# Moving the layer-embedding products of a two-block transformer kernel to the three row-norm places, unsplit, with the results parked in device memory

## The reference, cut to what matters

```
out = merged @ w_o
x = x + gate * rms_norm(out, g_post)
```

```
x = layer_norm(alpha * x + y, ln_g[i], ln_b[i])            # y = attention output @ w_out
x = x + (p[i] @ w_ple[i]) * sigmoid(x @ w_ple_gate[i])     # p[i]: 256 x 256, w_ple[i]: 256 x 2048
```

## Time and profile before

| what | value |
|---|---|
| median of 3 runs | 2474.22 us (2472.71 to 2475.14) |
| the profiled execution's own time | 2475.72 us |
| its span (first to last instruction) | 2474.4 us |
| PE busy | 2372.7 us (96%) |
| DVE busy | 1496.3 us (60%) |
| ACT busy | 1133.7 us (46%) |
| POOL busy | 110.6 us (4%) |
| mean granted PE clock | 0.986 |
| DMA, mean | 190 GB/s |

### The profile page before, as it was taken

One profiled execution on the slowest core, in us unless ns is written; L12 is line 12 of the kernel. 1 busy time (PEld: TensorE's weight loads), 2 busy tenths in 40 slices (PEclk: granted clock), 3 DMA queues, 4 the chain that ended last, 5 costly groups with the idle time before them and its releaser, 6 DMA issues.

```text
span 2474.4 us, 28104 instructions
## 1 busy us (share of the span) xinstructions
PE 2372.7 (96%) x11204; PEld 1974.9 (80%) x11204; DVE 1496.3 (60%) x2082; ACT 1133.7 (46%) x1482; POOL 110.6 (4%) x120
## 2 busy tenths in 40 slices
PE   7899999989999999999998999999899999999988
PEld 4577888878888887888887888888788888888867
DVE  6887665444545445776755685566655456456664
ACT  4233444434444454453344444554455545455343
POOL 1000000000000000000000000000100011011010
PEclk9999999999999999999998999999899999999999
DMA  8886544535553457887564545555456555555544
GB/s 348 323 312 244 170 140 127 158 128 188 188 191 113 139 177 246 296 291 255 170 195 148 166 159 171 159 161 186 157 181 193 167 173 170 182 163 171 198 149 151
DMA packets 133542, 470.56 MB, mean 190 GB/s; under 512 B 15537, under 2 KB 15793, under 8 KB 132385
## 3 DMA queue, kind: packets, MB, share of 16 engines
q1 hardware_dynamic: 130688, 458.42, 56.4%
q0 software_dynamic: 1424, 9.37, 1.0%
q10 hardware_dynamic: 1298, 0.97, 0.1%
HBM read 466.60 MB, written 2.10 MB: 189 GB/s over the span
## 4 chain that ended last, share of the span: by engine, by line
PE 80%; DVE 6%; ACT 3%; issue 1%; DMA 1%; POOL 0%; DVEq 0%; ACTq 0%
PE G L466 24%; PE G L468 24%; PE G L467 24%; PE A L541 4%; DVE wlo L378 2%; PE A L791 1%; PE A L815 1%; ACT whi L376 1%; ACT dil L496 1%; PE A L991 1%; DMA raw<-in_weights 0%; DVE dil L1729 0%; PE A L1456 0%; DVE CP L1735 0%; PE A L957 0%
## 5 line engine op out<-in xcount | busy, mean ns | idle before, releaser
L378 DVE TENSOR_TENSOR wlo<-raw,whi 128x1024 fp32r<-128x1024 f32 (+2 forms) x782 | 937.3, 1202 | 743.3 <-ACT whi L376 740.9
L376 ACT ACTIVATE whi<-raw 128x1024 fp32r<-128x1024 f32 (+2 forms) x782 | 800.5, 1026 | 852.4 <-PE G L468 739.4
L466 PE MATMUL G<-whi,XH 128*128 128x512 f32 (+3 forms) x2804 | 1091.0, 389 | 29.7 <-DVE wlo L378 13.3
L468 PE MATMUL G<-whi,XL 128*128 128x512 f32 (+3 forms) x2804 | 1070.6, 382 | 0.0
L467 PE MATMUL G<-wlo,XH 128*128 128x512 f32 (+3 forms) x2804 | 1069.8, 382 | 0.0
L466 PEld LDWEIGHTS G<-whi,XH 128*128 128x128 f32 x2804 | 529.6, 189 | 129.3 <-DVE wlo L378 19.1
L468 PEld LDWEIGHTS G<-whi,XL 128*128 128x128 f32 x2804 | 528.8, 189 | 95.9
L467 PEld LDWEIGHTS G<-wlo,XH 128*128 128x128 f32 x2804 | 529.9, 189 | 90.5 <-issue 0.5
L328 DVE CUSTOM_DVE_ANT_0 raw<-raw,dil 128x1024 f32<-128x1024 f32 x64 | 84.9, 1339 | 10.4 <-DMA raw<-in_weights 10.4
L466 PE MATMUL A<-whi,XH 128*128 128x512 f32 x164 | 70.0, 427 | 6.3 <-DVE XL L643 3.4
L468 PE MATMUL A<-whi,XL 128*128 128x512 f32 x164 | 64.6, 394 | 0.0
(11 more groups left out here) (195 smaller groups left out, 1621.0 us busy)
## 6 DMA issues: line engine op xcount, KB each, us to landing
raw<-in_weights SPq DMA_DIRECT2D x792, 512.0 KB, 4.2
raw<-in_weights SPq DMA_DIRECT2D x80, 384.0 KB, 3.1
raw<-in_weights SPq DMA_DIRECT2D x16, 288.0 KB, 2.9
raw<-in_weights SPq DMA_DIRECT2D x8, 336.0 KB, 3.0
FT<-in_xT SPq DMA_DIRECT2D x4, 512.0 KB, 5.6
Xn<-in_x POOLq DMA_DIRECT2D x1, 2048.0 KB, 11.8
GG<-in_ln_g POOLq DMA_DIRECT2D x2, 1024.0 KB, 8.4
CP<-in_ln_b POOLq DMA_DIRECT2D x2, 1024.0 KB, 5.1
```

The source lines that it names most:

```text
L376: th = AC.mark(nc.scalar.activation(h[:, 0:2 * cols], r[:, 0:2 * cols], ACT.Copy))
L378: tl = VE.mark(nc.vector.tensor_tensor(l[:, 0:2 * cols], r[:, 0:2 * cols], h[:, 0:2 * cols].bitcast(F32), ALU.subtract))
L466: nc.tensor.matmul(o, h, wh, start=(k == start), stop=False)
L468: ins = nc.tensor.matmul(o, l, wh, start=False, stop=(k == nkt - 1))
```

## The change

The eight embedding slots leave `ple`. Two are multiplied at row-norm place 0, three at place 1 and three at place 2 (layer 1's first chunk at place 1), in the unsplit form, with `p` transposed on the host (`pT`) as the left side. `fill` copies each result to a `nat` buffer (ACT), and POOL writes that to a buffer in device memory, `spill`; `nat_done` gets the token of this write. `fill_before` puts one slot (place 0) or two (places 1 and 2) ahead of the first transposes, and one behind the transposes of the first four tiles. `ple` has POOL load each chunk into `PL`. `p_task` and the load of `p` go away; `pT` (512 KB) is loaded by POOL behind three other loads after the first attention phase. The planner counts 3.45 us for an unsplit slot, also for those of before. POOL's descriptor scratch is set to 8192.

```diff
+    fills = deque((f"w_ple{layer}", 512 * c, 512, 2) for layer in range(2) for c in range(4))
+    plan_gemm([fills.popleft() for _ in range(2)])
     plan_gemm([("w_a", 5120, 384, KT), ("w_a", 5504, 384, KT), ("w_a", 5888, 336, KT), ("w_a", 2048, 512, KT),
...
     out_seq("w_oa")
+    plan_gemm([fills.popleft() for _ in range(3)])
     plan_gemm(ple_seq(0))
...
     out_seq("w_ob")
+    plan_gemm(fills)
     plan_gemm(ple_seq(1))
...
+        whole = WHOLE | {s for s, n in enumerate(wslots) if plan[n][1] in ("w_ple0", "w_ple1")}
...
-            PE.wait(loaded[n] if s in WHOLE else split_done[s])
+            PE.wait(loaded[n] if s in whole else split_done[s])
+            full, full_ready = (FT, whole_ready) if s in WHOLE else (xh, ready)
...
-            PE.busy(12 * (cols + 32) / 2400.0)
+            PE.busy(3.45 if s in whole else 12 * (cols + 32) / 2400.0)
...
+        pT = sb("pT", [128, 4, T], F32, px)
...
+        d_pT = load(GP, "pT", pT[:, :, :], i["pT"])
...
+        def fill(count):
+
+            for _ in range(count):
+                layer, c = fills.popleft()
+                pair, t = gemm(512, 2, pT[:, 2 * layer:2 * layer + 2, :], None, [d_pT, d_pT])
+                b, n, toks = nat_chunk(pair, t, 512)
+                GP.wait(*toks)
+                s = sem(f"d_spill{layer}{c}")
+                nc.gpsimd.dma_start(i["spill"][layer, c], b[:, :, :]).then_inc(s, 16)
+                spilled[(layer, c)] = (s, 16)
+                nat_done(n, spilled[(layer, c)])
+
+        def fill_before(tile, r, ahead, behind_it):
+
+            fill(ahead)
+            while r[tile] is None:
+                pump()
+            fill(behind_it)
...
+        fill_before(2, ready, 1, 1)
         pair0, t0 = gemm(384, KT, XH, XL, ready, look=2)
...
-        d_pp = load(GP, "pp", p_sb, i["p_2"].rearrange("l b (h p) n -> p (l b h) n", p=128))
...
-        quick.append(p_task())
...
             steps = new_x(norm_part, r)
             next(steps)
             quick.append(steps)
+            fill_before(2, r, 2, 1)
             return r
...
-                pair, t = gemm(512, 2, BH[:, 2 * layer:2 * layer + 2, :], BL[:, 2 * layer:2 * layer + 2, :],
-                               pready[layer])
                 b = PL
-                free["pl"] = [free.get("PT"), free.get("pl_used")]
-                toks = to_nat(b, pair, t, 512, "pl")
+                GP.wait(spilled[(layer, c)], free.get("PT"), free.get("pl_used"))
+                d_pl = load(GP, f"pl{layer}{c}", PL, i["spill"][layer, c])
+                toks = [d_pl, d_pl]
...
-    nc = bacc.Bacc("TRN2", target_bir_lowering=False, num_devices=1)
+    nc = bacc.Bacc("TRN2", target_bir_lowering=False, num_devices=1, dynamic_dma_scratch_size=8192)
```

More of the change, by code:

```diff
@@ L139, in ple_seq @@
     def ple_seq(layer):
[L140 to L143, removed]
+        return [(f"w_pg{layer}", 512 * c, 512, KT) for c in range(4)]
     def out_seq(w):
@@ L369, in emit_splits @@
                         return
-                    if s in WHOLE:
+                    if s in whole:
                         state["split"] += 1
@@ L440, in first_and_second_block @@
         x_read = [None] * KT
+        whole_ready = [None] * KT
         def gemm_slot(pair, cols, k0, nkt, xh, xl, ready, start=0, look=0):
@@ L453, in gemm_slot @@
                 k = k0 + kk
-                PE.wait(whole_ready[k] if s in WHOLE else ready[k])
+                PE.wait(full_ready[k] if s in whole else ready[k])
                 for hf in range(2):
                     o = pair[hf].t[:, 0:cols]
-                    if s in WHOLE:
-                        ins = nc.tensor.matmul(o, FT[:, k, hf * 128:(hf + 1) * 128],
+                    if s in whole:
+                        ins = nc.tensor.matmul(o, full[:, k, hf * 128:(hf + 1) * 128],
                                                in_raw(n)[:, kk * cols:(kk + 1) * cols],
@@ L619, in first_and_second_block @@
         ready = [None] * KT
-        whole_ready = [None] * KT
         first = [G[0:2], G[2:4]]
@@ L1294, in x_from_nat @@
                 r[k] = r[k + 1] = tk
+        fills = deque((layer, c) for layer in range(2) for c in range(4))
+        spilled = {}
+        def fill(count):
[13 more added lines that the diff above has]
+            fill(behind_it)
         bready = [bt_tok[k] for k in range(8)]
@@ L1387, in first_and_second_block @@
         buf2 = (S2, PT2, st2)
-        p_sb = E2[:, 0:1024].rearrange("p (h t) -> p h t", h=4)
         strict = masks[:, 1, :]
         d_strict = load(GP, "strict", strict, i["masks"][:, 4, :])
-        d_pp = load(GP, "pp", p_sb, i["p_2"].rearrange("l b (h p) n -> p (l b h) n", p=128))
         d_lg = load(GP, "lg0", LG[:, :], i["ln_g_2"][0:1, :].to_broadcast([128, D]))
@@ L1394, in first_and_second_block @@
         t_kzi = GP.mark(nc.gpsimd.memset(kzi, 0.0))
[L1395 to L1405, removed]
         def key_task(b, n, toks):
@@ L1783, in first_and_second_block @@
         pd.close()
-_INS = ["x", "c", "positions", "b_ada", "g_post", "g_kv", "p_2", "positions_2", "ln_g_2", "ln_b_2"]
+_INS = ["x", "c", "positions", "b_ada", "g_post", "g_kv", "positions_2", "ln_g_2", "ln_b_2"]
 def kernel(**inputs):
@@ L1800 @@
          np.asarray(inputs["c"])[0].reshape(KT, 128)], axis=0).T)
+    given["pT"] = np.ascontiguousarray(
+        np.asarray(inputs["p_2"])[:, 0].reshape(2, T, 2, 128).transpose(3, 0, 2, 1).reshape(128, 4, T))
     given["inv_freq"] = inverse_frequencies()
@@ L1806 @@
         aps[name] = nc.dram_tensor(f"in_{name}", a.shape, mybir.dt.from_np(a.dtype), kind="ExternalInput").ap()
+    aps["spill"] = nc.dram_tensor("spill", (2, 4, 128, 2, 512), F32, kind="Internal").ap()
     out = nc.dram_tensor("out_0", (1, T, D), F32, kind="ExternalOutput").ap()
```

## The result

The changed kernel takes 2448.84 us (median of 4 runs, 2445.88 to 2449.69) against 2474.68 before: ratio 0.9891, 95% interval 0.9879 to 0.9904. It is 25.8 us faster where 31 were forecast, inside the range of 2435 to 2456. Its profiled execution took 2449.69 us, its span is 2448.3. Two executions among those of the experiments, of 3433 and 8523 us, are counted in the medians there and not in the ratios.

The account below looks back on a forecast made before the run. PE was taken as the bound, carrying the chain for 80% of the span. Terms -16.4 - 10.0 - 4.4 - 3.7 + 0.3 + 3.4 = -30.8 us gave a predicted median of 2443.4 us, range 2435 to 2456.

Parts of the forecast that it names:

- p_task goes, -10.0: Near 1351 us, removing p_task saves PE's stall and low clock: -10.0 us, bounds -11.1 and -7.
- place 0's +0.2 against +0.3: At row-norm place 0, two fills use up the wait and the clock's loss: +0.3 us, bounds -1 and +3.
- Places 1 and 2, -4.4 and -3.7: First fill to second gate slot takes 15.7 us, against 20.1 and 19.45 before: -4.4 and -3.7 us.
- The new wait, +1.7 twice: At places 1 and 2, ACT's third-fill copy waits for POOL's first write, landing in 6.7 us: +1.7 us each.
- Embedding slots leave, -16.4: Six embedding slots of 2.73 us leave the gate products of chunks 1 to 3, two layers: -16.4 us.
- What was hidden beside them stays hidden: At chunk ends, DVE and ACT work stays covered, the next split being wanted two slots, 5.5 us, later.
- Costed at nothing: Fewer splits, PL loads, fill and gate weights, the pT load and smaller scratch add no time; planner shift allowed 1 us.
- No early reader: The pT load is one quarter of the loads queued ahead and nothing reads it early: costed at nothing.
- no fill ran at the low clock: Rival: the clock drops to 1.2 GHz during all eight fills, 28 us back, 2471 us; chance 0.06.
- No other wait of any size came at p_task's place: Rival: another wait, by the index rotation, replaces p_task's, up to 6 us, 2449 us; chance 0.08.
- POOL's writes landed in 6.0 us or less: Rival: POOL's queue bounds, slower beyond 20 us landings (2516 at 25); chance 0.03 for 12 to 20, 0.04 beyond.
- places 1 and 2 gained what was worked out: Rival: third fill or transposes fall in another order, places 1 and 2 gain nothing, 2451 us; chance 0.07.

Follow-up runs that it names:

- b2: Kernel before with POOL scratch 8192, p loaded early into its own buffer and p_task run behind the dilated products: 2469.92 us, ratio 0.998.
- e7: Changed kernel with all eight fills at place 0 and none at places 1 and 2: 2468.20 us, ratio 0.9972.
- e4: Changed kernel with its fills multiplied split, pT being split once behind the dilated products: 2455.27 us, ratio 0.9919.
- e6: Changed kernel with each fill's copy written two or four times, nat coming free with the last write: 2444.17 and 2463.08 us, one run each.
- e1: Changed kernel with the transposes of chunk 2's rows put two slots into chunk 3's gate product in layer 0: 2442.10 us, ratio 0.9874.
- e2: Changed kernel with only the load of pT issued later, after POOL waits for the last dilated gate product: 2445.28 us, ratio 0.9880.
- a0: The changed kernel run again with no edit: 2449.59 us, ratio to before 0.9896.
- b1: Kernel before with POOL scratch 8192 and p loaded early into its own buffer, p_task left in place: 2473.39 us, ratio 0.9992.

## Why the prediction came out as it did

*p_task goes, -10.0:* right in size. With place 0's +0.2 against +0.3 the two come to -9.4 behind the cut. (The bound of -7 does not follow from its own words: 11.1 less three times 1.1 is 7.8.) b2 gets 8.3 us behind the cut, and 4.8 in the median, by placing p_task elsewhere, so at least half of this third of the gain does not need the moved products.

*Places 1 and 2, -4.4 and -3.7:* right, -4.36 and -3.68; the tile was ready as worked out. e7 shows why it holds: the three fills stand wholly where PE would wait, and what left the path is the embedding slot that stood there. e4 shows the unsplit form to be needed for it: with split fills 4.1 and 3.7 us at the two places, nearly all of the gain there, are gone.

*The new wait, +1.7 twice:* the term was mis-sized, the mechanism was not. ACT does wait for the write, and the two e6 kernels agree with a price of L - 5, with the low clock on top where L is 10. But L was 3.1 us and not the 6.7 of the earlier trace rows. Why the write was quicker stays open: it is a write and that was a load, and the DMA engines had been idle ahead of it (share 0.00 from 1745 to 1750 us, 0.53 to 1755) where they were busy ahead of the load (0.68 from 1345.1 to 1350.1 us in the kernel before), while in the 5 us behind the issue both found them busy (0.84 and 0.86). No run varied one of these alone. The Trainium skill's estimate of 3.2 us (page "DMA: Bandwidth & Descriptors", section "Anatomy of one DMA — SWDGE (gpsimd) path") was the better one, and by it this write agrees: 3.1. The next two writes of the same place, of the same size, took 4.6 and 5.0.

*Embedding slots leave, -16.4:* the step that failed in part is "What was hidden beside them stays hidden". Five of six chunks gained 2.7 us. At chunk 3 of layer 0 `drain_all()` puts the transposes of chunk 2's rows right behind chunk 2's product. In the kernel before the embedding slot stood between, and PE still waited a little, by this row of its timeline, to which I gave no weight:

```profile
1847.46 1.06 PE L541 MATMUL A<-ident,Xn 128*128 128x128 f32 x8 [0.84 <-DVE Xn L1658]
```

0.84 + 2.73 = 3.57: the slot's whole length turned into the wait of 3.56, and the low clock behind it (0.66 from 1831 to 1836 us) cost 1.6 more. So 4.4 us of this term were lost, and e1 gets them back and one more. The prediction had looked for a late split there, not for the next transposes.

*Costed at nothing:* the loads of `PL`, the copies and the splits cost nothing that shows on the path: every chunk but 3 gained its whole slot. The load of `pT` did cost: 1.4 us in the changed kernel's two traces, about 3 in two others with the same instructions up to there. "No early reader" was true and beside the point: it delays the weight stream. The weight load that SP issued 8.9 us behind POOL's load of `x` landed in 13.1 us in the changed kernel, in 11.7 before and in 11.4 in e2.

*The sum:* -30.8, with 4.4 lost at chunk 3 and 3.4 not paid for the write, is -29.8; 29.3 was measured behind the cut. The median's 25.8 leaves 3.5 for what is ahead of it. In this pair of traces the 3.2 lost there can be placed: 1.4 at the load of `pT`, and 1.8 ahead of it, where the granted clock was low for longer (0.83 from 280 to 300 us and 0.80 from 485 to 520 in the changed kernel, 0.91 and 0.85 in the kernel before). These 1.8 are not the change's, since a0 has 0.91 and 0.85 with the same instructions. In the medians 1.4 to about 3 of the 3.5 can be `pT`'s; how often each price was paid in runs without a trace is not known, so the rest stays open.

*The rivals:* no fill ran at the low clock (1.00 in the stretches of all three places; the 6.15 us that priced this rival is itself a mixture, at 0.58 from 29 to 35 us). No other wait of any size came at p_task's place (0.37 and 0.27 us), POOL's writes landed in 6.0 us or less, and places 1 and 2 gained what was worked out.

## What to carry to other kernels

Before work is taken out from between a result and its reader, look for the reader's wait in the old trace: here even 0.8 us said that all of the removed time was cover, and it came back as a wait. Do not price a transfer by a row of the same size from another moment: here the same 512 KB landed in 20.1 or 4.7 us by the place of their issue alone. And cut both traces at the same instructions before comparing: here most parts behind the cut repeat to 0.1 us while whole runs scatter by 10.

## What the runs showed of the hardware

A 768-wide DVE split took 0.96 us alone and 3.01 to 3.06 beside POOL's 1.97 us of multiplies (3.06 in the changed kernel, where nothing waited for it). Taking POOL's multiply away restored 0.96. The Trainium skill (page "SBUF — State Buffer", section "SBUF: two separate sides") has a DVE instruction with two SBUF inputs and a GpSimd one that reads SBUF contend for a port pair, which the one that starts first holds for its whole instruction. The trace agrees in size, 3.01 - 0.96 being about the multiplies' length, but not in order: in b1's profile DVE's split starts 0.22 us ahead of POOL's first multiply and still is the one that grows. Spans on POOL are rough, so which of the two held the other up first is not shown.

The same wait was followed by different stretches of low clock: behind 3.56 us at chunk 3 the changed kernel lost 28.06 - 22.66 - 3.56 = 1.8 us and the kernel with two writes 2.9.
